# Triangular solve in blocks of 32 rows instead of 16, split into three parts, with unit preparation one query group sooner

## What is computed

```
m   = where(row > col, b * (K K^T) * decay, 0)        # strictly lower
sol = triangular_solve(m + I, [V * b, K * b * exp(g)])
for each chunk: v_new = u - w S;  o = q exp(g) S + (q k^T * decay) v_new;  S = S * decay + k^T v_new
```

## Time and profile before

| what | us |
|---|---|
| median of 3 runs | 2925.26 (2920.36 to 2925.65) |
| the profiled execution, its own time | 2924.31 |
| span of its profile | 2922.2 |
| PE busy | 2873.4 (98% of the span) |
| DVE busy | 1476.4 (51%) |
| POOL busy | 1371.2 (47%) |
| ACT busy | 987.4 (34%) |

### The profile page before, as it was taken

One profiled execution on the slowest core, in us unless ns is written; L12 is line 12 of the kernel. 1 busy time (PEld: TensorE's weight loads), 2 busy tenths in 40 slices (PEclk: granted clock), 3 DMA queues, 4 the chain that ended last, 5 costly groups with the idle time before them and its releaser, 6 DMA issues.

```text
span 2922.2 us, 46145 instructions
## 1 busy us (share of the span) xinstructions
PE 2873.4 (98%) x18742; PEld 2573.6 (88%) x18742; DVE 1476.4 (51%) x2410; ACT 987.4 (34%) x1470; POOL 1371.2 (47%) x1748
## 2 busy tenths in 40 slices
PE   9999999999999999999999999999999999999999
PEld 6778888877888889888899999999988799999999
DVE  6955322277522227996444544234897545444241
ACT  4443222255322233333443322224343434322221
POOL 5426554555655455432125555455442215555454
PEclk9989999999999999999999999999999999999999
DMA  5203333322333333222424233223322413323332
GB/s 177 65 22 101 101 94 94 94 95 77 98 100 94 94 95 122 95 72 85 107 70 138 81 94 90 91 86 96 102 73 67 120 62 123 100 88 93 95 91 69
DMA packets 124631, 271.24 MB, mean 93 GB/s; under 512 B 22808, under 2 KB 59032, under 8 KB 124184
## 3 DMA queue, kind: packets, MB, share of 16 engines
q1 hardware_dynamic: 73104, 246.05, 27.3%
q10 hardware_dynamic: 51336, 22.41, 2.8%
HBM read 250.35 MB, written 18.07 MB: 92 GB/s over the span
## 4 chain that ended last, share of the span: by engine, by line
PE 90%; DVE 6%; ACT 1%; issue 1%; ACTq 1%; DMA 0%; POOL 0%; DVEq 0%; POOLq 0%
PE acc L648 68%; PE acc L1024 5%; PE aux L1038 4%; PE acc L697 3%; PE acc L1005 2%; PE aux L1005 2%; DVE conv_out L2038 1%; PE aux L865 1%; PE acc L681 1%; PE aux L910 1%; PE acc L1038 1%; PE acc L1236 1%; PE aux L820 0%; PE aux L892 0%; PE acc L756 0%
## 5 line engine op out<-in xcount | busy, mean ns | idle before, releaser
L621 POOL TENSOR_TENSOR w_lo<-w_raw,w_hi 128x256 fp32r<-128x256 f32 x1744 | 1371.0, 818 | 1534.2 <-ACT w_hi L1270 1533.5
L648 PE MATMUL acc<-n_hi,w_hi 128*128 128x264 f32 (+1 forms) x3072 | 776.5, 314 | 5.2 <-POOL w_lo L621 3.6
L648 PE MATMUL acc<-n_lo,w_hi 128*128 128x264 f32 (+1 forms) x3072 | 767.6, 312 | 0.0
L648 PE MATMUL acc<-n_hi,w_lo 128*128 128x264 f32 (+1 forms) x3072 | 765.6, 311 | 0.0
L1270 ACT ACTIVATE w_hi<-w_raw 128x1024 fp32r<-128x1024 f32 (+1 forms) x436 | 455.4, 1045 | 686.9 <-PE acc L648 620.0
L648 PEld LDWEIGHTS acc<-n_hi,w_hi 128*128 128x128 f32 x3072 | 502.7, 188 | 56.8 <-issue 15.3
L648 PEld LDWEIGHTS acc<-n_lo,w_hi 128*128 128x128 f32 x3072 | 500.8, 188 | 34.3 <-issue 2.6
L648 PEld LDWEIGHTS acc<-n_hi,w_lo 128*128 128x128 f32 x3072 | 500.8, 188 | 31.5
L2140 DVE TENSOR_TENSOR x<-x,acc 128x512 f32<-128x512 f32 (+1 forms) x144 | 100.2, 695 | 571.0 <-PE acc L648 524.7
L648 PE MATMUL acc<-hidden_lo,w_hi 128*128 128x264 f32 (+1 forms) x1216 | 345.3, 331 | 0.0
L648 PE MATMUL acc<-hidden_hi,w_hi 128*128 128x264 f32 (+1 forms) x1216 | 345.2, 331 | 0.0
(11 more groups left out here) (480 smaller groups left out, 3744.2 us busy)
## 6 DMA issues: line engine op xcount, KB each, us to landing
w_raw<-in_stream SPq DMA_DIRECT2D x420, 512.0 KB, 3.6
unit_blocks<-unit_scratch ACTq DMA_DIRECT2D x30, 256.0 KB, 4.9
w_raw<-in_stream SPq DMA_DIRECT2D x16, 384.0 KB, 3.0
unit_scratch<-unit_staged ACTq DMA_DIRECT2D x20, 256.0 KB, 2.8
saved_x<-x SPq DMA_DIRECT2D x2, 2112.0 KB, 8.8
x<-saved_x SPq DMA_DIRECT2D x16, 264.0 KB, 2.7
saved_gates<-root ACTq DMA_DIRECT2D x12, 264.0 KB, 2.1
unit_scratch<-unit_staged ACTq DMA_DIRECT2D x1, 2560.0 KB, 13.5
```

Of the source, the lines that this page charges most:

```text
L621: i = pool.tensor_tensor(wl[:, slot, s], raw[:, slot, s], wh[:, slot, s].bitcast(F32), ALU.subtract)
L648: last = pe.matmul(o, w[:, p % W_SLOTS, P * b:P * b + P], r, start=(b == 0 and i == 0), stop=(b == n - 1 and i == 2))
```

## The change

Blocks have 32 rows, so there are 64 blocks of units 1 to 4 and 4 of unit 0, one per partition, on 68 partitions, 1024 numbers each and 31 rows to solve. The join levels go from three to two. The solve is cut in three: start and rows 0 to 9 at the end of j = 2, rows 10 to 15 two at a time behind the shifts of heads 0 to 2 of j = 3, rows 16 to 23 behind the last normalisation of j = 3, and rows 24 to 30 with the transposing copy behind the taking of piece z 0. For this all units are prepared one place sooner (1 and 2 around the end of j = 0, 3 and 4 around the end of j = 1), and `fetch_blocks` moves from head 1 of j = 3 to head 2 of j = 2. The fills are dealt out anew: slot 0 gets 4 more blocks behind its transposes, slots 1 to 4 one fewer each. The buffers of the solve move, and with them DVE's wait for `solved_sent`: it now stands ahead of the unit stage.

```diff
-FILL = [[8, 0, 0, 0, 0, 0, 0]] + [[1, 1, 1, 2, 1, 1, 1]] * 4 + [[2, 1, 2, 0, 0, 0, 3]]
-SCORE_FILL = [[1, 2, 1, 0], [2, 2, 2, 2], [3, 2, 1, 0], [2, 2, 2, 2]]
-TAKEN_BEFORE = [3, 4, 3, 4]
-EARLY, NEXT_UNIT = {2: 3}, (1, 2, 4)
+FILL = [[8, 4, 0, 0, 0, 0, 0], [1, 1, 1, 1, 1, 2, 0], [1, 1, 1, 1, 1, 2, 0], [1, 1, 1, 1, 1, 1, 1], [1, 1, 1, 1, 1, 2, 0],
+        [2, 1, 2, 0, 0, 0, 3]]
+SCORE_FILL = [[1, 2, 1, 0], [3, 2, 1, 0], [3, 2, 1, 0], [2, 2, 2, 2]]
+TAKEN_BEFORE = [3, 3, 3, 4]
+EARLY, NEXT_UNIT = {1: 2, 2: 4}, {0: 1, 1: 3}
...
-SMALL = 16
-LEVELS = (4, 5, 6)
+SMALL = 32
+LEVELS = (5, 6)
+LAST = len(LEVELS) - 1
+SOLVED = 4 * A_HEADS * (P // SMALL)
+SOLVES = SOLVED + A_HEADS
+SOLVE_BEGIN, SOLVE_HEADS, SOLVE_BREAK = 10, 2, 24
...
PE, slot(s):
             fill(FILL[s][3])
+            if v >= 0:
+                step_out(v)
             if joined:
                 join_half(u, 1)
             fill(FILL[s][4])
             if joined:
                 join(u, 1)
-            if v >= 0:
-                step_out(v)
-            if joined:
-                join_half(u, 2)
             fill(FILL[s][5])
-            if joined:
-                join(u, 2)
             fill(FILL[s][6])
...
ACT, slot(s): the copy for the third half and gap(5) go; gap(5) stands before gap(6)
ACT, attention():
                 if j in EARLY:
                     decays(EARLY[j])
                     decay_steps(EARLY[j])
-                    send(2)
-                    send(3)
+                    send(EARLY[j] - 1)
+                    send(EARLY[j])
                 if j == 3:
-                    send(4)
                     c.next(unit_made, UNITS)
...
-                    if j == 3 and h == 1:
+                    if j == 2 and h == 2:
                         fetch_blocks()
...
DVE, filler and layer:
-                    if m == 5:
-                        dve.wait_ge(solved_sent, 64 * (l + 1))
...
             attention(l, filler)
+            dve.wait_ge(solved_sent, 64 * (l + 1))
             step(dve.memset(decayed, 0.0))
...
DVE, the solve:
+        def solve_start(l):
+
+            flat = solved[0:SOLVES].rearrange("p r c -> p (r c)")
+            step(dve.memset(flat, 0.0))
             dve.wait_ge(*c.mine())
+            step(dve.memset(flat[:, ::SMALL + 1], 1.0))
             dve.wait_ge(blocks_landed, 32 * (l + 1))
+
+        def solve_rows(a, z):
+
+            for j in range(a, z):
                 n = SMALL - 1 - j
+                shape = [SOLVES, n, j + 1]
...
+                dve.wait_ge(*c.mine())
                 dve.wait_ge(*step(dve.tensor_tensor(
...
+                step(dve.tensor_tensor(rows, rows, t, ALU.subtract))
+
+        def solve_end(l):
+            dve.wait_ge(*c.mine())
+            dve.wait_ge(bo_full, 5 * (l + 1))
+            dve.tensor_copy(turned[0:SOLVES], solved[0:SOLVES].rearrange("p r c -> p c r"))\
+                .then_inc(blocks_solved, c.made(blocks_solved))
...
DVE, slot(s): join_block(2) and the second joined_both() go; gap(5) stands before gap(6)
DVE, attention():
                     shift(j, h)
                     if h:
                         normalise(j, h - 1)
+                    if j == 3 and h < 3:
+                        solve_rows(SOLVE_BEGIN + SOLVE_HEADS * h, SOLVE_BEGIN + SOLVE_HEADS * (h + 1))
...
                 normalise(j, B_HEADS - 1)
+                if j in NEXT_UNIT:
+                    prepare(NEXT_UNIT[j], l)
+                if j == 2:
+                    solve_start(l)
+                    solve_rows(0, SOLVE_BEGIN)
                 if j < 3:
-                    prepare(NEXT_UNIT[j], l)
                     filler(*ATTN_FILLERS[2 * j + 1])
                 if j + 1 in EARLY:
                     prepare(EARLY[j + 1], l)
             c.next(bt_full, 5)
-            dve.wait_ge(gate_sent, c.at(gate_sent))
-            solve_blocks(l)
+            solve_rows(SOLVE_BEGIN + 3 * SOLVE_HEADS, SOLVE_BREAK)
             filler(*ATTN_FILLERS[7])
+            solve_rows(SOLVE_BREAK, SMALL - 1)
+            solve_end(l)
```

More of the change, by code:

```diff
@@ L379, in build @@
     ik = rest.take("index_k", [P, T])
+    bv = rest.take("attn_v", [P, T])
     bk = rest.take("attn_k", [P, T])
-    bv = rest.take("attn_v", [P, T])
     selb = rest.take("select_bias", [P, SEL_AT[4]])
@@ L391, in build @@
     meta_p = rest.take("meta_probs", [P, B_HEADS, META])
+    products = rest.take("solve_products", [P, SMALL * SMALL // 4])
     glast = rest.take("chunk_decay", [P, UNITS, A_HEADS])
@@ L406, in small_tiles @@
     def small_tiles(a):
-        return a[:, 0:2 * SMALL * SMALL].rearrange("p (s r c) -> p s r c", s=2, r=SMALL)
+        return a[:, 0:SMALL * SMALL].rearrange("p (r c) -> p r c", r=SMALL)
     states = [four(ssq[:, :]), four(sqb[:, 0, :])]
@@ L416, in build @@
     dt = [four(ub[:, 0, :]), four(ub[:, 1, :])]
-    lt, solved, turned, products = small_tiles(ik[:, :]), small_tiles(rt[:, :]), small_tiles(ub[:, 1, :]), small_tiles(bv[:, :])
+    lt = Area(nc, W + 3 * TILES4, end).take("solve_blocks", [P, SMALL, SMALL])
+    solved, turned = (small_tiles(a[:, :, :].rearrange("p s t -> p (s t)")) for a in (sqb, sb_))
     gates = [ub[:, 0, :], ub[:, 1, :], sb_[:, 0, :], sb_[:, 1, :]]
@@ L426, in small_blocks @@
     def small_blocks(kind, u):
-        n, step = (P, 1) if u else (A_HEADS, P // SMALL)
+        n, step = (SOLVED, 1) if u else (A_HEADS, P // SMALL)
         return bass.AP(scratch, kind * KIND_PITCH + u * UNIT_PITCH, [[step * BLOCK_PITCH, n], [P, SMALL], [1, SMALL]])
@@ L1078, in join @@
                 pe.wait_ge(vb_ready, c.next(vb_ready, A_HEADS))
-            if n < 2:
+            if n < LAST:
                 heads(aux[:, 0, :], lambda o, h: mm_(o, y_in[:, h, :], p1[:, h, :]))
@@ L1239, in attention @@
                         mm.then_inc(bo_full, 1)
-                    if v == 0 and j < 3:
+                    if v == 0 and j in NEXT_UNIT:
                         prepare_queries(NEXT_UNIT[j])
@@ L1759, in fetch_blocks @@
             act.wait_ge(unit_sent[1], c.next(unit_sent[1], 32 * 2))
[L1760 to L1761 removed]
+            act.dma_start(lt[SOLVED:SOLVES, :, :], small_blocks(M_PART, 0)).then_inc(blocks_landed, 16)
+            act.dma_start(lt[0:SOLVED, :, :], small_blocks(M_PART, 1)).then_inc(blocks_landed, 16)
         def send_solved():
@@ L1765, in send_solved @@
             for part, t in ((X_PART, solved), (Y_PART, turned)):
-                act.dma_start(small_blocks(part, 0), t[0:A_HEADS, 1, :, :]).then_inc(solved_sent, 16)
-                act.dma_start(small_blocks(part, 1), t[:, 0, :, :]).then_inc(solved_sent, 16)
+                act.dma_start(small_blocks(part, 0), t[SOLVED:SOLVES, :, :]).then_inc(solved_sent, 16)
+                act.dma_start(small_blocks(part, 1), t[0:SOLVED, :, :]).then_inc(solved_sent, 16)
         def fetch_unit(u, parts=(M_PART, X_PART, Y_PART)):
@@ L1817, in slot @@
             gap(4)
-            gap(5)
-            if joined:
-                half(aux[:, 0, :])
             if v >= 0:
@@ L1836, in slot @@
                 out_roots()
+            gap(5)
             gap(6)
@@ L1888, in attention @@
                         .then_inc(bt_ready, c.made(bt_ready))
-                    if b == 1 and j < 3:
+                    if b == 1 and j in NEXT_UNIT:
                         decay_steps(NEXT_UNIT[j])
@@ L1897, in attention @@
                     .then_inc(bo_ready, c.made(bo_ready))
-                if j < 2:
-                    send(j)
+                if j == 0:
+                    send(0)
                 if j < 3:
@@ L2735, in slot @@
                 join_block(1)
-                join_block(2)
             gap(2)
@@ L2743, in slot @@
             gap(4)
-            if joined:
-                dve.wait_ge(*written)
-                written = joined_both()
-            gap(5)
             if v >= 0:
@@ L2779, in normalise @@
                     .then_inc(bp_ready, c.made(bp_ready))
-            step(dve.memset(ik[:, SMALL * SMALL:2 * SMALL * SMALL], 0.0))
             dve.wait_ge(bs_full, c.next(bs_full))
```

20 lines of the change are left out of this document (6 added, 14 removed).

## The result

| what | before | after |
|---|---|---|
| median of 11 runs each, us | 2925.88 (2920.36 to 2927.58) | 2933.26 (2928.71 to 2937.5) |
| after / before | | 1.0025 (95%: 1.0017 to 1.0033) |
| the profiled execution, its own time, us | 2924.31 | 2933.54 |
| its span, us | 2922.2 | 2931.7 |

The kernel is 0.25% slower, 7.4 us. The forecast was 2926 and no change; the measured time lies inside the range, near its upper end. It is at the edge of the 0.2% that separate no change from slower: the interval reaches from 0.17% to 0.33%.

The account below looks back on a forecast made before the run. PE bounds the kernel, busy 2873.4 of 2922.2 us. Per layer, gains of 12.9 less costs of 12.25 and 1.0 for the clock give -0.35, twice 0.7 us more: 2926 us, no change (chance 0.47), range 2915 to 2935.

Parts of the forecast that it names:

- join level, surcharges, 0.56 and 0.43: Per layer: one join level less in four units 11.1, four lone-block surcharges 0.8, PE waits in slot 1 and j = 1.
- shifts and piece of j = 3: Rows 10 to 15 between the shifts delay the taking of the piece behind them; PE waits 2.2 us longer a layer.
- tail of the solve and write, slot 0: Late rows 24 to 30 and copy delay `w_and_u(0)`: 4.65 a layer net of four blocks, plus 0.8 for larger written packets.
- keys of unit 4 moved, j = 2: Behind the last head's scores, PE without these keys reaches the transposes 1.6 us too soon and waits, per layer.
- Y in slot 2: Piece z 2 ends earlier, ACT's work for it precedes the squares, and PE waits 2.1 us for Y in `w_and_u`.
- slot 3: Gate 6 ends at the sixth fill place; the next piece begins at once and waits for its taking, 0.9 us a layer.
- clock: PE's new waits in j = 3, slot 0 and slot 2 may lower its clock: 0 to 5.1 us a layer, taken as 1.0.
- output products too early for the copy: Slots 1 to 4: output products in the removed level's place, counted only as removing slot 1's 0.56 wait; no wait costed.
- The solve: On DVE, 23.5 us where 11 stood; rows 0 to 9 and 16 to 23 hidden, the other stretches delay PE.
- The rival that it would not bite: Faster, chance 0.27: ACT's order in slot 2 costs nothing, clock holds, only late-solve waits are real; 2919.8 or 2915.
- the second rival: Slower, chance 0.26: clock falls behind j = 3, slot 0 and slot 2, 5.1 us a layer, 2934; two places give 2931.

Follow-up runs that it names:

- the mended kernel: Changed kernel with copy ahead of subtractions, squares ahead of slot 2's piece, solve rows 0 to 11 first, one row a head, rest ahead of z 0: 2903.56, 0.9928.

## Why the prediction was right or wrong

The sum of the prediction, per layer, beside what the traces show (first and second layer where they differ; gains positive, us):

| step | predicted | measured |
|---|---|---|
| join level, surcharges, 0.56 and 0.43 | +12.9 | in place: 192 instructions gone, both waits gone |
| shifts and piece of j = 3 | -2.2 | -2.5 (0.76 + 0.67 + 1.98 - 0.91) |
| tail of the solve and write, slot 0 | -5.45 | -5.2, -5.5 (from z 0 to `w_and_u(0)` 17.88 against 9.73 before, 18.11 against 9.70; less the four blocks, 2.95) |
| keys of unit 4 moved, j = 2 | -1.6 | -1.24 (0.77 + 0.47) |
| Y in slot 2 | -2.1 | -2.1 |
| slot 3 | -0.9 | -0.96 |
| clock | -1.0 | -1.26, and +1.64 in the second layer |
| output products too early for the copy | 0 | -3.55 (0.87 + 1.34 + 1.34) |

With the 12.9 taken as predicted, the last column gives -3.9 in the first layer and -2.6 in the second, 6.5 together; the traces are 4.14 and 2.16 apart, 6.3 together. The sum is less exact than this looks, since two errors in it nearly cancel: the level brought some 1.5 a layer more than the prediction gave it (next paragraph), and the waits for the copy cost 4.3 a layer and not their bare 3.55, as the run with the copy first shows.

**The level.** Right, and a little low. The earlier trace rows gave the price of each instruction, 23.8 for both layers with the surcharges; the mended kernel, whose stages have as much time at the lower clock as before, is busy 26.8 less.

**The solve.** Right where PE waits for it. Rows 14 and 15 go at 0.455 from start to start (predicted 0.46), the copy took 1.11 (1.15), the solve ends 6.08 behind the taking of z 0 (6.15). `w_and_u(0)` comes 12.65 behind the end of the solve (12 to 13). Two stretches that are hidden ran longer than predicted, rows 0 to 9 for 7.8 instead of 6.8 and rows 16 to 23 for 8.5 instead of 7.0; the last section shows why. It cost PE nothing there: DVE still waited 1.35 for the piece behind the first and 5.59 for z 0. The chain on DVE and on ACT, changed kernel, answering to the earlier trace rows:

```profile
1421.93 0.71 DVE L2494 TENSOR_TENSOR delta_z<-acc,norm_scale 128x528 f32<-128x528 f32 x1 [5.59 <-PE acc L1031]
...
1426.90 1.11 DVE L2674 COPY unit_b<-squares 68x1024 f32<-68x1024 f32 x1
1434.11 0.48 DVE L2499 MEMSET squares<- 128x512 f32 x1 [6.09 <-DMA unit_scratch<-unit_b]
```

```profile
1428.05 0.27 ACTq L1769 DMA_DIRECT2D unit_scratch<-squares  x1
...
1430.73 0.60 ACT L1895 ACTIVATE attn_out<-acc 128x512 f32<-128x512 f32 x1 [11.38 <-issue]
...
1435.57 1.06 ACT L1273 ACTIVATE w_hi<-w_raw 128x1024 fp32r<-128x1024 f32 x1 [4.24 <-issue]
```

From the first issue of the write to ACT's next split it is 1435.57 - 1428.05 = 7.52, where the kernel before has 6.90 (1411.98 to 1418.88). In the second layer it is 7.63 against 6.85. So the packets of double size cost 0.6 to 0.8; the prediction had 0.8, and had kept 3.5 as the upper end. Nearly all of it stands between the first issue and the attention output, where ACT issues the writes (2.68 against 2.02). By the cycles that the Trainium skill ("DMA: Bandwidth & Descriptors", Why small descriptors are slow) gives a packet, it would have been 1.4, as an estimate; the measurement decides.

**j = 2, slot 2, slot 3.** Right within 0.4 each. In slot 2 the order on ACT was the reason, as the run with the squares first shows. The rival that it would not bite is out.

**The clock.** In this trace the level fell at two of the three places of the second rival, behind j = 3 and over slot 0, and not behind slot 2. (It did fall behind slot 2's wait in one layer each of the second profile of the same kernel and of the runs with the whole solve ahead of z 0 and with rows 10 to 15 cut to three.) That is the point from which the prediction let the slower rival decide. But the price was smaller than the rival's 1.7 a place: 1.26 behind j = 3, and in slot 0 nothing that can be seen, because PE waited for ACT there. The prediction took the drop behind `w_and_u(0)` in the kernel before as a cost; in the first layer it was none: from `w_and_u(0)` to the state product of slot 1, which needs `v_new`, it takes 5.52 in both kernels, and where PE ran slowly it waited 0.46 for `v_new`, and where it ran fast 2.06. Only in the second layer of the kernel before, where the drop came behind that wait, did it cost 1.64 (13.30 against 11.66 from there to the third half of slot 1), and the changed kernel does not have it there. Over both layers the clock is about 0.9 in all, not 2.0.

**The step that failed** is one that the prediction put at nothing without a reason. It counted the output products in slots 1 to 4 as a gain ("the output products now stand in that place") and looked at what they cover, not at what they wait for. What stands ahead of a moved step on every engine was asked for the solve, the fills and the keys, and not for this one. On DVE the copy out of the same bank stands behind two subtractions that wait for PE; that order was harmless where the products stood before. PE's waits for it are 3.55 a layer, 7.1 us in all, which is about the difference between the 0.7 predicted and the 7.4 measured; with what they cost beyond their length it is 8.6, and the level's surplus takes the rest back. That it is the cause, and not only beside it, is shown by the run that exchanges the two statements (2921.71, wait gone, nothing in its place). That the move was otherwise right is shown by the run that takes it back (2933.15; if the move brought nothing, it would have been 2921.71).

So the forecast of no change came from a nearly right sum with one term missing, and the slower rival, which gave its time by the clock, would have been right for a reason that is not the main one. That the result lies in the range is luck in this respect: the upper end was drawn for the clock, and what filled it was a wait that was not in the sum.

Open is why each wait for the copy costs some 0.25 us more than its length, and why the clock falls behind j = 3 in some layers and not in others that have the same waits. And the change with 32-row blocks but the units prepared as before was not tried.

## What to carry to other kernels

When a step is moved earlier on the engine that bounds, list for each of its operands and its output buffer the instruction that frees it on the other engines, and what stands in front of that one in its own queue; here one copy of 0.22 to 0.68 us behind two subtractions of 0.68 made the whole difference between 1.0029 and 0.9995. Small instructions that release a waiting engine go ahead of larger ones that wait themselves, and long serial work of a side engine is best cut to fit that engine's measured idle (DVE's 5.59 us ahead of z 0), before the taking for which the main engine waits rather than behind it, with a little slack (filled to the end it cost 0.7 at z 0). A change that brings nothing can be a good one in the wrong order: the same join level gave 0.9928 once three orders were mended.

## What the runs showed of the hardware that was not expected

DVE's small products and subtractions of the solve took 0.4 to 0.5 us longer while POOL was at work, which doubles the large ones and triples the smallest. Timeline of DVE, changed kernel:

```profile
1385.16 0.67 DVE L2669 TENSOR_TENSOR squares<-squares,solve_products 68x31 f32<-68x31 f32 x1
...
1407.86 0.42 DVE L2666 TENSOR_TENSOR solve_products<-solve_blocks,squares 68x255 f32<-68x255 f32 x1
1408.32 0.84 DVE L2669 TENSOR_TENSOR squares<-squares,solve_products 68x255 f32<-68x255 f32 x1
1409.19 0.83 DVE L2666 TENSOR_TENSOR solve_products<-solve_blocks,squares 68x252 f32<-68x252 f32 x1
...
1411.77 0.41 DVE L2669 TENSOR_TENSOR squares<-squares,solve_products 68x247 f32<-68x247 f32 x1
...
1426.68 0.19 DVE L2669 TENSOR_TENSOR squares<-squares,solve_products 68x31 f32<-68x31 f32 x1
```

and of POOL:

```profile
1407.99 3.48 POOL L628 TENSOR_TENSOR w_lo<-w_raw,w_hi 128x256 fp32r<-128x256 f32 x4 [10.12 <-ACT w_hi L1273]
```

Of the rows 16 to 23 the slow ones are those that start between 1407.99 and 1411.47, and only those. The slow one of 68 x 31 at 1385.16 lies in POOL's work from 1383.66 to 1386.46 (0.67), and its like at 1426.68 has no POOL work beside it (0.19). The Trainium skill ("GPSIMD Engine Reference", Specifications) says that the two engines contend for SBUF where a DVE instruction has two inputs there; these products and subtractions have both inputs in SBUF, and the trace agrees, 0.83 against 0.41 for like sizes. It is one more reason for leaving slack where such work has to fit between the takings of pieces. What it cost PE here was not measured by itself: the second of the two waits of j = 3 (0.67) came without any POOL work, the first (0.76) with it.
